# A two-layer hybrid decoder: five reorderings of work around the state-space mixer and the experts

## The chip, the cores and the metric

One Trainium2 chip, one core of it. The metric is the device time of one execution in microseconds. The kernel before takes 1630.93 us, the median of three runs.

## What is computed

A decoder trunk of two layers on 256 tokens of width 1024, in float32. The change touches the second layer, a Mamba-2 mixer and a top-2-of-8 expert layer:

```python
def mamba2_mixer(x, w_in, conv_w, conv_b, dt_bias, a_log, d_skip, norm_w, w_out):
    z, xbc, dt = split_last(x @ w_in, (SSM_D_INNER, SSM_CONV_DIM, SSM_HEADS))
    xbc = jax.nn.silu(causal_depthwise_conv(xbc, conv_w) + conv_b)
    xs, bmat, cmat = split_last(xbc, (SSM_D_INNER, SSM_GROUPS * SSM_STATE, SSM_GROUPS * SSM_STATE))
    ...
    dt = jax.nn.softplus(dt.astype(f32) + dt_bias)
    y = ssd_chunked(xs, dt, -jnp.exp(a_log.astype(f32)), ...)
    y = y + d_skip.astype(f32)[:, None] * xs.astype(f32)
    y = y.reshape(Bsz, T, SSM_D_INNER) * jax.nn.silu(z.astype(f32))
    y = rms_norm(y.reshape(Bsz, T, SSM_GROUPS, -1), norm_w.reshape(SSM_GROUPS, -1)).reshape(Bsz, T, SSM_D_INNER)
    return y.astype(x.dtype) @ w_out
```

The scan runs over two chunks of 128 tokens and four groups of 8 heads. Behind it stand a layer norm, the router, and eight SwiGLU experts of width 3584 whose rows are picked per token.

## The kernel before, in words

Each engine has one instruction stream written out by hand, and the streams wait for one another through semaphores; there is no scheduler. The order in which an engine's work stands in the source is the order in which it runs.

**Weights.** Weights come in pieces of 1 MB (128 x 2048 floats). SP loads a piece into one of six or seven buffers `raw`; ACT casts it to the fp32r type, `w_hi` (`dense_high`, L690); DVE subtracts to make the low half, `w_lo` (`dense_low`, L1112); PE multiplies three times, high by high, high by low, low by high. Three pairs of `w_hi` and `w_lo` exist in the mixers (`CUT`), so ACT may cast piece n once piece n-3 is used (`d_piece_used`), and SP may load piece n once the low half of piece n-6 is made (`d_lo_made`, `RAW_D`). In the experts there are four pairs (the fourth lies in `xT_hi` and `xT_lo`) and seven buffers; there the cast is L936, the low half L1551, the products L2318 to L2320.

**Input projection (`PROJ`, 20 pieces from N1).** Per piece PE runs 48 matmuls of 256 columns (`columns`, L1810 to L1812). Twelve pieces (kind 0) are followed by a depthwise convolution on DVE (L1137, L1141) and a SiLU on ACT (L861), eight (kind 1, the gate) by a SiLU on ACT alone (L864). The order of kinds is 0, 0, 1, 0, 1, four times over. At step 8 (`ACS_AT`) PE sums the decays over the tokens, into bank 7. DVE takes them out of that bank (L1432, L1433, `nacs` and `sdd`), at its own step 8, ahead of that step's low half; PE must not write bank 7 in step 9 before that (`ssm_cols`).

**Scan.** For eight pairs (chunk t, group g) PE makes rows of decay sums (`acs_rows`, L2192 and L2195), ACT their exponentials (`segments`, L881), DVE the product with the chunk's C B matrix (L1477), PE the y of the group (`y_products`, L2207), DVE adds the skip term (L1458) and, in chunk 0, the gate (L1467). ACT copies four states (L892) between the exponentials of groups 0 and 1. Ahead of all that ACT's stream issues two DMAs that fill the slot arrays `x_slots` (4 MB) and `y_slots` (2.5 MB) in DRAM with zeros (L885, L887); only POOL's scatter of tokens, some 130 us later, needs them. DVE makes the low half of the first piece of the output projection, N2, ahead of the product of the third pair.

**Output projection (eight pieces from N2).** For chunk 1 four groups of offsets come from PE (`offset_products`, L2219 and L2221), ACT (`offset_decay`, L902) and DVE (`offset_add`, L1485 to L1490). ACT scales and casts y (`y_high`, L907) and squares it (`y_square`, L914); DVE makes the low part (`y_low`, L1495) and folds the squares (`over_chunks`, L1516, L1517). Two pieces make one group; `y_out(i, t)` is piece i for token tile t, 12 matmuls of 512 columns (L2248 to L2250), and a group's result takes four banks, 4 to 7 for groups 0 and 2, 0 to 3 for groups 1 and 3. The squares are summed by 16 small matmuls (L2260); DVE makes the mean (L1527), POOL its power -1/2 (L649), and DVE adds each group, scaled, to `x_tok` (`group_add`, L1504). In the kernel before PE sums the squares behind group 0 and waits for the mean before group 1, since the sums lie in bank 0. Behind `out_tile` DVE begins the layer norm.

**Experts.** DVE works out each token's slot in the arrays (L1680 to L1692) ahead of the low half of the first expert's fifth piece; POOL scatters the tokens by it (L656, four indirect DMAs), and the other experts read their tokens from `x_slots` (L987). Each expert has seven steps of gate, up and down product; `turn_h` (L2343) transposes h, ACT and DVE copy it as high and low (L969, L1600), `down` multiplies. In the last expert the last `turn_h` stands behind the last but one `down`.

## Time and profile before

| | |
|---|---|
| median of 3 runs | 1630.93 us (1630.56 to 1632.22) |
| profiled execution, its own time | 1623.04 us |
| its span | 1621.2 us |
| PE busy | 1570.1 us, 97% |
| weight loads of PE | 1331.7 us, 82% |
| DVE busy | 1281.6 us, 79% |
| ACT busy | 967.3 us, 60% |
| POOL busy | 54.8 us, 3% |
| moved by DMA | 459.39 MB, 283 GB/s over the span |

Busy time of an engine counts its instructions, not its waits. In the timelines a row is one or several instructions of a line, with start and duration in us; in brackets stand the engine's idle time just before and the instruction that ended it. The granted clock is given as a share of 2.4 GHz; 0.5 is 1.2 GHz. The input projection of the state-space mixer lies at 394 to 522 us, its scan to 570, its output projection to 629, layer norm and router to 650, the experts to 1609.

### The profile page before, as it was taken

What the parts mean: (1) busy time and instruction counts of PE and PEld (TensorE: products, weight loads), DVE (VectorE), ACT (ScalarE), POOL (GpSimd) and SP (SyncE); (2) the same over time, 40 slices, a digit from 0 to 9 for tenths busy, and PEclk for the clock granted to TensorE, in tenths of its full rate; (3) what the DMA queues carried; (4) which work ended last, traced back from release to release, by engine and by line L of the source; (5) the groups of instructions that cost most, each with busy time, mean ns of one, the idle gap of its engine ahead of it and who ended that gap; (6) DMA issues with size and microseconds to landing.
All of it is one profiled execution on the core that took longest, in us unless ns stands there. A gap on an engine that the chain in (4) does not pass through costs nothing.

```text
span 1621.2 us, 22157 instructions
## 1 busy us (share of the span) xinstructions
PE 1570.1 (97%) x8631; PEld 1331.7 (82%) x8631; DVE 1281.6 (79%) x1059; ACT 967.3 (60%) x821; POOL 54.8 (3%) x43
## 2 busy tenths in 40 slices
PE   9989999999989899999999999999999999999996
PEld 7888599998989777788888878888878888888885
DVE  6776545557667587988888888888888889888996
ACT  4414244443434552777777777777767777777773
POOL 3000000002000010100000000000000000000100
PEclk9999999999999999999999999999999999999998
DMA  9150365554543506899999999999999999999991
GB/s 322 61 197 1 128 191 185 194 184 139 173 145 142 196 27 236 308 394 394 395 390 388 381 370 367 384 377 394 376 377 367 386 374 386 387 382 378 393 397 68
DMA packets 221758, 459.39 MB, mean 283 GB/s; under 512 B 7684, under 2 KB 64736, under 8 KB 221664
## 3 DMA queue, kind: packets, MB, share of 16 engines
q1 hardware_dynamic: 208800, 434.95, 73.8%
q10 hardware_dynamic: 11152, 18.42, 3.1%
q0 software_dynamic: 1712, 4.68, 0.8%
q8 instruction: 70, 1.15, 0.3%
q14 instruction: 24, 0.20, 0.0%
HBM read 444.38 MB, written 13.63 MB: 283 GB/s over the span
## 4 chain that ended last, share of the span: by engine, by line
PE 87%; DVE 8%; ACT 2%; issue 1%; ACTq 1%; POOL 0%; DMA 0%; DVEq 0%; SPq 0%
PE ps L2318 19%; PE ps L2320 19%; PE ps L2319 19%; PE ps L1810 5%; PE ps L1811 5%; PE ps L1812 5%; PE ps L1803 2%; PE ps L2343 2%; DVE w_lo L1112 1%; PE ps L2089 1%; PE ps L2090 1%; PE ps L2091 1%; DVE arena L1141 1%; ACT w_hi L690 1%; PE ps L2009 1%
## 5 line engine op out<-in xcount | busy, mean ns | idle before, releaser
L1551 DVE TENSOR_TENSOR w_lo<-raw,w_hi 128x2048 fp32r<-128x2048 f32 x252 | 576.9, 2291 | 71.6 <-ACT w_hi L936 70.7
L936 ACT CAST w_hi<-raw 128x2048 fp32r<-128x2048 f32 x252 | 482.8, 1916 | 132.7 <-PE ps L2320 132.7
L2318 PE MATMUL ps<-w_hi,xg_hi 128*128 128x512 f32 x672 | 267.8, 399 | 6.6 <-DVE w_lo L1551 3.6
L2320 PE MATMUL ps<-w_hi,xg_lo 128*128 128x512 f32 x672 | 262.6, 391 | 0.0
L2319 PE MATMUL ps<-w_lo,xg_hi 128*128 128x512 f32 x672 | 261.8, 390 | 0.0
L1112 DVE TENSOR_TENSOR w_lo<-raw,w_hi 128x2048 fp32r<-128x2048 f32 (+1 forms) x72 | 170.1, 2367 | 112.3 <-ACT w_hi L690 112.3
L1810 PE MATMUL ps<-xT_hi,w_hi 128*128 128x256 f32 x768 | 219.9, 286 | 7.1 <-DVE arena L1433 6.8
L690 ACT CAST w_hi<-raw 128x2048 fp32r<-128x2048 f32 (+1 forms) x72 | 135.3, 1881 | 147.5 <-PE ps L1812 97.1
L1811 PE MATMUL ps<-xT_lo,w_hi 128*128 128x256 f32 x768 | 219.3, 286 | 0.0
L1812 PE MATMUL ps<-xT_hi,w_lo 128*128 128x256 f32 x768 | 219.1, 285 | 0.0
L1551 DVE TENSOR_TENSOR xT_lo<-raw,xT_hi 128x2048 fp32r<-128x2048 f32 x84 | 192.4, 2290 | 30.3 <-ACT xT_hi L936 30.3
L936 ACT CAST xT_hi<-raw 128x2048 fp32r<-128x2048 f32 x84 | 160.8, 1915 | 43.8 <-PE ps L2320 43.8
L1810 PEld LDWEIGHTS ps<-xT_hi,w_hi 128*128 128x128 f32 x768 | 149.2, 194 | 8.6 <-DVE arena L1433 7.0
L2318 PEld LDWEIGHTS ps<-w_hi,xg_hi 128*128 128x128 f32 x672 | 126.3, 188 | 32.4 <-issue 7.5
L1811 PEld LDWEIGHTS ps<-xT_lo,w_hi 128*128 128x128 f32 x768 | 149.2, 194 | 0.4
L1812 PEld LDWEIGHTS ps<-xT_hi,w_lo 128*128 128x128 f32 x768 | 149.3, 194 | 0.0
L2320 PEld LDWEIGHTS ps<-w_hi,xg_lo 128*128 128x128 f32 x672 | 126.2, 188 | 27.3
L2319 PEld LDWEIGHTS ps<-w_lo,xg_hi 128*128 128x128 f32 x672 | 126.6, 188 | 24.4
L2318 PE MATMUL ps<-w_hi,ehT_hi 128*128 128x512 f32 x336 | 131.6, 392 | 1.4 <-DVE ehT_lo L1600 1.4
L2319 PE MATMUL ps<-w_lo,ehT_hi 128*128 128x512 f32 x336 | 130.9, 390 | 0.0
L2320 PE MATMUL ps<-w_hi,ehT_lo 128*128 128x512 f32 x336 | 130.9, 390 | 0.0
L2320 PE MATMUL ps<-xT_hi,xg_lo 128*128 128x512 f32 x224 | 87.3, 390 | 0.0
(396 smaller groups left out, 2165.8 us busy)
## 6 DMA issues: line engine op xcount, KB each, us to landing
raw<-in_moe_w_gate SPq DMA_DIRECT2D x112, 1024.0 KB, 7.6
raw<-in_moe_w_up SPq DMA_DIRECT2D x112, 1024.0 KB, 8.3
raw<-in_moe_w_down SPq DMA_DIRECT2D x112, 1024.0 KB, 8.1
raw<-in_ssm_w_in SPq DMA_DIRECT2D x20, 1024.0 KB, 5.3
raw<-in_ffn_w_gate SPq DMA_DIRECT2D x11, 1024.0 KB, 5.4
raw<-in_ffn_w_up SPq DMA_DIRECT2D x11, 1024.0 KB, 5.4
raw<-in_ffn_w_down SPq DMA_DIRECT2D x11, 1024.0 KB, 4.9
raw<-in_even_w_in SPq DMA_DIRECT2D x10, 1024.0 KB, 13.2
```

The lines of the kernel that those rows point to most:

```text
L690: act.copy(w_hi[:, c, 0:size], raw[:, i, 0:size]).then_inc(sem("dense_hi_made"), 1)
L936: act.copy(e_hi((n + 2 * odd) % CUT_E), raw[:, i, :]).then_inc(sem("hi_made"), 1)
L1112: TTO(w_lo[:, c, 0:size], raw[:, i, 0:size], w_hi[:, c, 0:size].bitcast(F32), ALU.subtract).then_inc(d_lo_made, 1)
L1551: TTO(e_lo(c), raw[:, n % RAW, :], e_hi(c).bitcast(F32), ALU.subtract).then_inc(lo_made, 1)
L1803: last = mm(ps[:, 4 + 2 * t + n, :], mixT[:, k, t * P:(t + 1) * P], w[:, kk, 512 * n:512 * n + 512], start=k == 0, stop=k == KD - 1)
L1810: mm(out_ap, whi, xT_hi[:, k, :], start=first, stop=False)
L1811: mm(out_ap, whi, xT_lo[:, k, :], start=False, stop=False)
L1812: return mm(out_ap, wlo, xT_hi[:, k, :], start=False, stop=last_)
L2318: mm(out_ap, hi, whi, start=start, stop=False)
L2319: mm(out_ap, hi, wlo, start=False, stop=False)
L2320: return mm(out_ap, lo, whi, start=False, stop=stop)
L2343: last = pe.transpose(ps[:, 4, c * P:(c + 1) * P], eh[:, side(j), c * P:(c + 1) * P], ident)
```

## The change

Five things change places; no instruction that computes is added or taken away.

1. DVE takes the column sums out of bank 7 at its step 6 (`COLS_AT`), behind that step's low half.
2. The two clears are issued by SP, behind the sixth load of the output projection, and not by ACT.
3. In the output projection ACT casts pieces N2+1 and N2+2 earlier, the first ahead of all offsets; DVE makes their low halves earlier, folds all squares in one lot, makes the mean, and interleaves the low halves N2+3 and N2+4 with the y low parts of groups 2 and 3. PE runs `y_out(2, 0)` ahead of the sums of squares, which now go to bank 3, and waits for the mean only before the second half of `y_out(2, 1)`.
4. The 15 operations of the slot arithmetic go into the first expert's head in three lots, at its steps 12, 15 and 18 (`slot_rows`, `slot_numbers`, `slot_weights`: the same 15 lines, parted).
5. In the last expert the last `turn_h` stands between the two halves of the last but one `down` (`turn_next`, set for that one alone).

```diff
-DT_AT, SP_AT, DA_AT, ACS_AT = 3, 5, 6, 8
+DT_AT, SP_AT, DA_AT, COLS_AT, ACS_AT = 3, 5, 6, 6, 8
@@ stream of SP @@
             for i in range(N_OUT):
                 n = N2 + i
                 piece(n, n % RAW_D, rows(w_out1, 2 * i, 2))
+                if i == RAW_D - 1:
+                    sp.wait_ge(sem("pool_set"), 2)
+                    sp.dma_start(x_slots[0:E * P, :].rearrange("(p r) (s c) -> p (r s) c", p=P, c=256),
+                                 zerob[:, :].bitcast(F32).unsqueeze(1).to_broadcast([P, 4 * E, 256])).then_inc(sem("slots_cleared"), 16)
+                    sp.dma_start(y_slots[(E - 1) * P:, :].rearrange("(p r) (s c) -> p (r s) c", p=P, c=256),
+                                 zerob[:, :].bitcast(F32).unsqueeze(1).to_broadcast([P, 4 * (1 + 2 * TT), 256])).then_inc(sem("slots_cleared"), 16)
@@ stream of ACT, ahead of the scan @@
-            act.wait_ge(sem("pool_set"), 2)
-            act.dma_start(x_slots[0:E * P, :]
...
-            act.dma_start(y_slots[(E - 1) * P:, :]
@@ stream of ACT, output projection @@
+            act.wait_ge(sem("y_made"), SG)
+            act.wait_ge(sem("xdec_made"), 1)
+            out_high(N2 + 1)
             offset_decay(0)
             offset_decay(1)
             y_high(0)
             y_square(0)
             offset_decay(2)
             y_high(1)
-            out_high(N2 + 1)
             offset_decay(3)
+            act.wait_ge(sem("y_made"), TT * SG)
+            out_high(N2 + 2)
             y_square(1)
             y_high(2)
+            y_square(2)
             y_high(3)
-            y_square(2)
             y_square(3)
-            out_high(N2 + 2)
@@ stream of DVE, input projection @@
-                if m == ACS_AT:
+                n = N1 + m + CUT
+                if n < N2:
+                    dense_low(n, n % RAW_D, n % CUT)
+                if m == COLS_AT:
                     dve.wait_ge(sem("acs_made"), 1)
                     link(TS(nacs[:, :, :], ps[:, 7, 64:64 + TT * SH].rearrange("p (t h) -> p t h", t=TT), -1.0, None, ALU.mult))
                     TTO(sdd[:, :], ps[:, 7, 128:160], nacs[:, 0, :], ALU.add).then_inc(sem("ssm_cols"), 1)
-                n = N1 + m + CUT
-                if n < N2:
-                    dense_low(n, n % RAW_D, n % CUT)
@@ stream of DVE, output projection @@
             offset_add(2)
+            dve.wait_ge(sem("yoff_made"), SG)
+            out_low(N2 + 1)
             offset_add(3)
             y_low(1)
-            out_low(N2 + 1)
...
-            over_chunks(0)
-            over_chunks(1)
+            out_low(N2 + 2)
+            for g in range(SG):
+                over_chunks(g)
+            dve.wait_ge(sem("y_ss"), 1)
+            TS(ymean[:, :], ps[:, 3, 0:TT * SG], 1.0 / (SI // SG), RMS_EPS, ALU.mult, ALU.add).then_inc(sem("y_mean"), 1)
+            out_low(N2 + 3)
             y_low(2)
-            over_chunks(2)
-            over_chunks(3)
+            out_low(N2 + 4)
             y_low(3)
-            out_low(N2 + 2)
-            dve.wait_ge(sem("y_ss"), 1)
-            TS(ymean[:, :], ps[:, 0, 0:TT * SG], 1.0 / (SI // SG), RMS_EPS, ALU.mult, ALU.add).then_inc(sem("y_mean"), 1)
...
+            dve.wait_ge(sem("y_rn"), 1)
+            add_group(0)
+            out_low(N2 + 5)
+            out_low(N2 + 6)
+            dve.wait_ge(sem("y_summed"), 1)
+            add_group(1)
+            out_low(N2 + 7)
@@ stream of DVE, experts @@
-            def expert_head(it, odd, previous, previous_e, back=False):
+            def expert_head(it, odd, previous, previous_e, back=False, first=False):
                 for n in range(START, HEAD_END):
+                    if first and n == START + 8:
+                        slot_rows()
+                    if first and n == START + 11:
+                        slot_numbers()
+                    if first and n == START + 14:
+                        slot_weights()
@@ stream of PE, output projection @@
                 if g == 1:
                     pe.wait_ge(sem("yoff_added"), 4)
+                    y_out(2, 0)
                     pe.wait_ge(sem("ysq_summed"), SG)
                     for t in range(TT):
                         for q in range(SG):
-                            last = mm(ps[:, 0, SG * t + q:SG * t + q + 1], ysq[q][:, t * P:(t + 1) * P], ones[:, 0:1],
+                            last = mm(ps[:, 3, SG * t + q:SG * t + q + 1], ysq[q][:, t * P:(t + 1) * P], ones[:, 0:1],
                                       start=True, stop=True)
                     last.then_inc(sem("y_ss"), 1)
-                    pe.wait_ge(sem("y_mean"), 1)
+                    y_out(2, 1, True).then_inc(d_piece_used, 1)
+                    y_out(3, 0)
+                    y_out(3, 1).then_inc(d_piece_used, 1)
                 if g >= 2:
                     pe.wait_ge(sem("y_summed"), g - 1)
-                if g < SG - 1:
+                if g in (0, 2):
@@ stream of PE, experts @@
                 for half in range(PPU):
+                    if half and turn_next:
+                        turn_h(it, j + 1)
                     pe.wait_ge(lo_made, count(PPE, it, (RAW + n + half + 1)))
...
                 else:
-                    turn_h(it, ESTEPS - 1)
                     down(it, odd, ESTEPS - 1, place(ESTEPS - 1, 2, False), by_half)
```

Three places in the order of the instructions follow, where parts 1 to 3 lie.

DVE in the input projection, before: from the low half of piece N1+9 (step 6) to the convolution of step 8. L1112 is a low half, L1137 and L1141 a convolution, L1432 and L1433 the column sums.

```order
L1112 TENSOR_TENSOR w_lo<-raw,w_hi 128x2048
L1137 TENSOR_SCALAR arena<-ps,pcol 128x256 x2
L1141 SCALAR_TENSOR_TENSOR arena<-ps,pcol,arena 128x255 x2
L1141 SCALAR_TENSOR_TENSOR arena<-ps,pcol,arena 128x254 x2
L1141 SCALAR_TENSOR_TENSOR arena<-ps,pcol,arena 128x253 x2
L1112 TENSOR_TENSOR w_lo<-raw,w_hi 128x2048
L1432 TENSOR_SCALAR arena<-ps 128x64
L1433 TENSOR_TENSOR arena<-ps,arena 128x32
L1112 TENSOR_TENSOR w_lo<-raw,w_hi 128x2048
L1137 TENSOR_SCALAR arena<-ps,pcol 128x256 x2
```

And in the change, where the same lines are L1116, L1141 and L1145, L1439 and L1440:

```order
L1116 TENSOR_TENSOR w_lo<-raw,w_hi 128x2048
L1439 TENSOR_SCALAR arena<-ps 128x64
L1440 TENSOR_TENSOR arena<-ps,arena 128x32
L1141 TENSOR_SCALAR arena<-ps,pcol 128x256 x2
L1145 SCALAR_TENSOR_TENSOR arena<-ps,pcol,arena 128x255 x2
L1145 SCALAR_TENSOR_TENSOR arena<-ps,pcol,arena 128x254 x2
L1145 SCALAR_TENSOR_TENSOR arena<-ps,pcol,arena 128x253 x2
L1116 TENSOR_TENSOR w_lo<-raw,w_hi 128x2048 x2
L1141 TENSOR_SCALAR arena<-ps,pcol 128x256 x2
```

The two rows of the sums moved from behind the second low half to behind the first, ahead of the convolution.

ACT from the copies of the chunk products to the exponentials of the scan, before (L885 and L887 are the clears, L892 the copies of the states):

```order
L872 COPY arena<-ps 128x512 x2
L885 DMA x_slots<-zerob 4096x1x256
L887 DMA y_slots<-zerob 2560x1x256
L881 ACTIVATE arena<-ps,arena 128x128 x8
L892 COPY arena<-ps 128x512 x4
L881 ACTIVATE arena<-ps,arena 128x128 x8
L690 CAST w_hi<-raw 128x2048
L881 ACTIVATE arena<-ps,arena 128x128 x48
```

In the change, and on to the first offsets (L696 is a weight cast, L903 an offset's exponential):

```order
L878 COPY arena<-ps 128x512 x2
L887 ACTIVATE arena<-ps,arena 128x128 x8
L893 COPY arena<-ps 128x512 x4
L887 ACTIVATE arena<-ps,arena 128x128 x8
L696 CAST w_hi<-raw 128x2048
L887 ACTIVATE arena<-ps,arena 128x128 x48
L696 CAST w_hi<-raw 128x2048
L903 ACTIVATE arena<-ps 128x512 x2
L908 ACTIVATE y_hi<-arena,pcol 128x256 x4
```

The clears left ACT's stream, and a weight cast came in between the scan's exponentials and the offsets'.

DVE in the output projection, before, from the fold of the third square to the addition of group 0 (L1495 is y low, L1527 the mean, L1504 the addition):

```order
L1516 TENSOR_TENSOR arena<-arena 128x512
L1517 TENSOR_TENSOR arena<-arena 128x256
L1516 TENSOR_TENSOR arena<-arena 128x512
L1517 TENSOR_TENSOR arena<-arena 128x256
L1495 SCALAR_TENSOR_TENSOR xT_lo<-arena,pcol,y_hi 128x256 x4
L1112 TENSOR_TENSOR w_lo<-raw,w_hi 128x2048
L1527 TENSOR_SCALAR arena<-ps 128x8
L1112 TENSOR_TENSOR w_lo<-raw,w_hi 128x2048 x2
L1504 SCALAR_TENSOR_TENSOR x_tok<-ps,arena,x_tok 128x1024 x2
```

In the change (L1499 is y low, L1527 the mean, L1508 the addition):

```order
L1512 TENSOR_TENSOR arena<-arena 128x512
L1513 TENSOR_TENSOR arena<-arena 128x256
L1512 TENSOR_TENSOR arena<-arena 128x512
L1513 TENSOR_TENSOR arena<-arena 128x256
L1527 TENSOR_SCALAR arena<-ps 128x8
L1116 TENSOR_TENSOR w_lo<-raw,w_hi 128x2048
L1499 SCALAR_TENSOR_TENSOR xT_lo<-arena,pcol,y_hi 128x256 x4
L1116 TENSOR_TENSOR w_lo<-raw,w_hi 128x2048
L1499 SCALAR_TENSOR_TENSOR xT_lo<-arena,pcol,y_hi 128x256 x4
L1508 SCALAR_TENSOR_TENSOR x_tok<-ps,arena,x_tok 128x1024 x2
```

The mean now stands ahead of two low halves and two y low parts that stood in part ahead of it, and the addition of group 0 right behind them.

## Rows read from the trace of the kernel before

**Rows 1.** Busy time by stretch: us, PE, PEld, DVE, ACT, POOL (instructions), PEclk, DMA share, GB/s
```profile
456.00:464.00 8.00, 7.45 (x45) 7.45 (x46) 6.06 (x12) 1.00 (x3) 0.00 (x0) 0.67 0.83 262
...
480.00:522.00 42.00, 42.00 (x352) 42.00 (x352) 30.74 (x46) 15.91 (x19) 0.00 (x0) 1.00 0.43 151
...
586.00:594.00 8.00, 7.46 (x28) 6.06 (x28) 7.86 (x18) 4.12 (x4) 0.00 (x0) 0.79 0.40 131
...
660.00:680.00 20.00, 16.45 (x75) 13.28 (x73) 19.75 (x17) 12.60 (x9) 7.74 (x4) 1.00 0.81 296
...
680.00:700.00 20.00, 20.00 (x92) 16.58 (x91) 18.45 (x10) 14.80 (x10) 0.00 (x0) 1.00 1.03 396
```

**Rows 2.** Timeline of PE at its waits: start us, us, operation [idle before <-releaser]
```profile
456.55 0.58 PE L1810 MATMUL ps<-xT_hi,w_hi 128*128 128x256 f32 x1 [6.76 <-DVE arena L1433]
...
541.05 1.97 PE L2207 MATMUL ps<-arena 128*64 128x128 f32 x16 [5.26 <-ACT arena L892]
...
586.53 0.47 PE L2248 MATMUL ps<-w_hi,y_hi 128*128 128x512 f32 x1 [1.80 <-DVE w_lo L1112]
...
664.42 0.47 PE L2318 MATMUL ps<-w_hi,xg_hi 128*128 128x512 f32 x1 [3.55 <-DVE w_lo L1551]
...
1600.28 0.50 PE L2318 MATMUL ps<-w_hi,ehT_hi 128*128 128x512 f32 x1 [1.40 <-DVE ehT_lo L1600]
```

**Rows 3.** Timeline of DVE in the state-space input projection
```profile
447.50 0.87 DVE L1137 TENSOR_SCALAR arena<-ps,pcol 128x256 f32<-128x256 f32 x2
...
483.17 0.87 DVE L1137 TENSOR_SCALAR arena<-ps,pcol 128x256 f32<-128x256 f32 x2
...
489.53 4.58 DVE L1112 TENSOR_TENSOR w_lo<-raw,w_hi 128x2048 fp32r<-128x2048 f32 x2 [2.77 <-ACT w_hi L690]
```

**Rows 4.** Timeline of ACT behind the copies of the chunk products
```profile
528.65 8.10 ACTq L887 DMA_DIRECT2D y_slots<-zerob  x1
```

**Rows 5.** Timeline of ACT, DVE and PE, second and third scan group
```profile
540.70 2.28 ACT L881 ACTIVATE arena<-ps,arena 128x128 f32<-128x128 f32 x8
...
543.01 1.23 DVE L1477 TENSOR_TENSOR arena<-arena 128x1024 f32<-128x1024 f32 x1 [2.78 <-ACT arena L881]
...
546.03 2.29 DVE L1112 TENSOR_TENSOR w_lo<-raw,w_hi 128x2048 fp32r<-128x2048 f32 x1
...
550.58 1.10 PE L2207 MATMUL ps<-arena 128*64 128x128 f32 x16 [0.18 <-DVE arena L1477]
```

**Rows 6.** Timeline of PE, DVE and POOL in the output projection
```profile
579.00 0.50 PE L2248 MATMUL ps<-w_hi,y_hi 128*128 128x512 f32 x1
...
588.43 1.66 DVE L1495 SCALAR_TENSOR_TENSOR xT_lo<-arena,pcol,y_hi 128x256 fp32r<-128x256 f32 x4
...
593.69 0.50 PE L2260 MATMUL ps<-ones,raw 128*128 128x1 f32 x4
...
596.16 5.84 POOL L649 TENSOR_TENSOR arena<-arena,nhalf 128x8 f32<-128x8 f32 x1 [195.82 <-DVE arena L1527]
...
623.77 1.28 DVE L1504 SCALAR_TENSOR_TENSOR x_tok<-ps,arena,x_tok 128x1024 f32<-128x1024 f32 x1 [3.06 <-PE ps L2250]
```

**Rows 7.** Timeline of DVE ahead of the first expert
```profile
656.80 0.17 DVE L1680 SCALAR_TENSOR_TENSOR rowf<-const,rank 128x16 f32<-128x16 f32 x1
...
659.89 0.17 DVE L1693 TENSOR_SCALAR rank<-rank 128x16 f32<-128x16 f32 x1
```

**Rows 8.** DMA issues, 600 to 720 us: KB each, us to landing; the first token load
```profile
raw<-in_moe_w_gate SPq DMA_DIRECT2D x12, 1024.0 KB, 12.0
...
x_slots<-x_tok,slot_of POOLq DMA_INDIRECT x4, 8.7
...
L987 ACTq DMA_DIRECT2D xg_tok<-x_slots x7: 362/366/367, 732.2 to 1446.2; - x7
```

**Rows 9.** Timeline of DVE and PE at the end of the last expert
```profile
1594.53 0.68 DVE L1596 TENSOR_TENSOR eh<-esg,ps 128x512 f32<-128x512 f32 x1
...
1598.28 0.60 PE L2343 MATMUL ps<-const,eh 128*128 128x128 f32 x4
```

More of the change, by code:

```diff
@@ L2412, in expert_rest @@
                         (turn_tokens if placed else gather)(following)
-                    down(it, odd, j - 1, place(j - 1, 2))
+                    if following is None and j == ESTEPS - 1:
+                        down(it, odd, j - 1, place(j - 1, 2), False, None, True)
+                    else:
+                        down(it, odd, j - 1, place(j - 1, 2))
                     if place(j - 1, 2) + 1 == PLACE_G and not placed:
```

66 lines of the change are left out of this document (30 added, 36 removed).

## Prediction

> **What bounds the kernel now.** I read the busy time by stretch first. Through the projections TensorE is busy for the whole of a stretch [rows 1]: from 480 to 522 us it runs 352 matmuls of 256 columns in 42.00 us, 0.12 us each, so a piece of the projection (48 matmuls) is 5.76 us. So only what holds PE up, or lowers its clock, is worth anything, and I went to its timeline next [rows 2]: five waits of more than a microsecond from 450 us on, each ended by another engine, none by a DMA. Each of the five parts of the change lies at one of them. Then I read what the releasing engine did just before [rows 3 to 9]. The profiled execution took 1623.04 us (span 1621.2); the median of the runs is 1630.93, 7.9 us or 0.5% more, and I subtract the same sum from it. A measurement of this kernel tells 0.2%, 3.3 us, from no change.
>
> **Part 1, the column sums ahead of the convolutions (COLS_AT).** Piece 9 of the projection waits 6.76 us for L1433 [rows 2], since DVE computes it two steps late. In the stretch behind, the granted clock is 0.67 of 2.4 GHz over 8 us [rows 1]: 2.6 us lost, 2.3 of them in matmuls. Loss 9.1 us. In the change DVE does the sums right behind the low half of piece 9, at 447.50 [rows 3], 0.45 us of work for which everything is there, and PE goes on at 449.8. But DVE and ACT hold a loop of their own: convolution, SiLU, cast of the next piece, low half. It takes 6.36 us from the start of a convolution to the next low half (483.17 to 489.53) [rows 3] and 2.2 for that low half (4.58 for two); with a gate piece between, another 2.2 to 2.3. A group of five pieces (three convolutions) so takes the loop 30.3 us and PE 28.8, so the loop decides where PE gains its lead. From 447.95 the low half of piece 10 ends at 447.95+6.36+2.2 = 456.5, PE wants it at 455.5: 1.1 with the signal. The convolutions of pieces 8, 10 and 11 then start at 458.8, 469.65 (10.85 each, with a gate piece between) and 478.2 (8.56), the low half of piece 15 ends at 478.2+8.6 = 486.8, and PE wants it at 456.6 + 5 x 5.76 = 485.4: 1.4. **Part 1 gives 9.1 - 1.1 - 1.4 = 6.6 us.** Bounds: 9.1 if no wait returned, 5 if the loop is 0.5 us slower at each turn.
>
> **Part 2, clearing the slot arrays from SP's queue.** ACT's queue is held for 8.10 us by the issue of the second clear [rows 4]; the exponentials and the state copies stand behind it, and PE waits 5.26 us for the copies [rows 2]. PE had finished the second group's row sums at 535.79. Without the clears ACT's exponentials of group 1 start then, not at 540.70, and take 2.2; DVE's product (543.01 before) starts at 538.15. From that product to PE's third group nothing waits for long: product, additions, gate, the low half of out-piece 0 at 546.03, the next product, 6.5 us in all. So the third group starts at 544.65 and not at 550.58 [rows 5]. **Part 2 gives 5.9 us**, with the half clock there in it. The groups behind keep their spacing, which PE's own work sets. A new PE wait of about 1.9 us stands before the third group: PE has two groups' row sums and two products to do from 535.79, some 6.9 us as I estimate from its work between the waits, and the low half is now late relative to it. On SP the clears go behind the sixth out-piece, issued when the last projection piece's low half is done (some 509 us in the new time). SP is held about 9 us, and its next load needs the low half of out-piece 0, at least 20 us later; the transfers (6.5 MB) lie beside PE work that needs no load. Cost nothing; without that cover, the 9 us.
>
> **Part 3, the output projection.** From 579.00 to the layer norm at 623.77 are 44.8 us [rows 6]. Ten half pieces (12 matmuls) fill 596.2 to 623.6: 2.73 us each. The change casts piece 1 while ACT waited for the offset products, so the wait of 1.80 us for its low half [rows 2] goes, and with it the fall of the clock behind it: 0.79 over 8 us, 3.4 us at 1.2 GHz, 1.7 lost [rows 1]. PE now runs five half pieces (13.65 us) before the sums of squares. From their start, 2.4 us to the mean. DVE then stands before low 3, y low, low 4, y low, addition of group 0: 2.2+1.6+2.2+1.6+2.4 = 10.0 (y low is 1.66, an addition 1.28 a tile) [rows 3, 6], and PE may overwrite group 0's banks 12.5 us after the sums began. It has 1.8 + 3 x 2.73 = 10.0 us of work till then: **a new wait of 2.5 us**. Six half pieces follow, 16.4. Sum 13.65+12.5+16.4+0.2 = 42.8: **part 3 gives 2.0 us**. The mean's power on POOL takes 5.84 us [rows 6]; DVE asks for it 7.6 us after the mean, 1.6 to spare.
>
> **Part 4, the slot arithmetic behind eight pieces of the first expert.** PE waits 3.55 us for the low half of piece 4 [rows 2]. Ahead of it on DVE stand 15 small operations from 656.80 to 659.89 [rows 7]: **3.1 us**, all less than the wait. They come back in three lots, at most 1.5 us, where DVE is idle 1.55 of 20 us [rows 1] and a low half is finished some 4 us before PE takes it. POOL's scatter of the tokens moves from 661 to about 697 us, where the DMA engines are full (share 1.03, 396 GB/s). It writes 2.1 MB, 5.3 us of their time. A load is issued when the low half seven pieces back is done, and its cast starts when the piece four back is used: 7 x 2.8 - 4.2 = 15.4 us, against 12.0 to landing [rows 8]; with the 4 us behind the cast that is 7.4 of slack, so I take nothing. Bounds: 0 and 3.1 lost.
>
> **Part 5, the last transposes between the halves of the last but one product.** After them (1598.28) PE waits 1.40 us for ACT and DVE [rows 2]; now 2.73 us of matmuls lie over that chain. DVE has multiplied the h that they read by 1595.2 [rows 9], and they now come at 1598.28 - 2.73 = 1595.55. **1.4 us**; bounds 1.4 and, if h came later than they do, some tenths less.
>
> **Sum:** 6.6 + 5.9 + 2.0 + 3.1 + 1.4 = 19.0 us. What I take off again is the clock. PE has two new waits, 1.9 and 2.5 us. The old one of 1.80 us was followed by 3.4 us at 1.2 GHz (0.79 in rows 1), the one of 3.55 us was not (1.00 from 660 to 680 us), so either can happen, and I count one of two: 1.7 us. That gives 17.3 us: 1605.7 for a profiled execution, **1613.6 for the median**. [...]
>
> **The rivals.**
> *No fall of the clock behind either new wait*: 19.0 us, 1611.9. For it: the 3.55 us wait. Chance 0.25.
> *Both fall*: 15.6 us, 1615.3. For it: the 1.80 us wait; the first of the new ones lies among short matmuls. 0.15.
> *The gain ahead of the first expert is lost*: scatter and weight loads share full DMA engines and the casts come late, or the lots of small operations delay the low halves. The 5.3 us of the scatter must exceed the slack of 7.4; I may have that slack too large by the few microseconds that loads are late at the start. Time 1613.6 + 3.1 = 1616.7. 0.08. [...]
> *The change moves waits and shortens nothing (1630.9)*: the loop of DVE and ACT would have to take back all of part 1, the third scan group all of part 2. The rows give it 2.5 of 9.1 and 1.9 of 8. 0.03.
> *Slower*: ACT waits at the end of the first expert's first half until all four scatters have landed; the token load behind that wait was issued at 732.2 [rows 8], in the new time near 729 of the old scale. The scatters start near 697, POOL needs 7.7 us for them (rows 1, 660 to 680), and a landing took 8.7: 714, 15 us ahead. Beyond 729 each microsecond stops the casts, and PE with them once its few ready pieces are used. It decides from 15 + 17 = 32 us of added landing time; a landing of 60 us in place of 8.7 would make 1613.6 + 51 - 15 = 1650. No kind of transfer in rows 8 takes more than 12 in the median. 0.02.
>
> **How the numbers follow.** The forecast itself, one of the two falls, has 0.43; 0.04 is left for a gain smaller than all but the last rivals, from a step I mis-sized. The range goes from 1610.6 (no fall, and 1.3 us of rounding in the parts) to 1618.2 (both falls with nearly all of part 4 lost, or part 1 at its lower bound with one fall and part 4 lost). Faster by over 0.2% is the forecast, the first three rivals and the leftover: 0.95. Same 0.03, slower 0.02.
>
> **What would show it.** In the profile after: no PE wait for the column sums, but one near piece 10 and one near piece 15 of the projection, 1.1 and 1.4 us; the projection ends 6 to 7 us earlier; the clear's issue on SP and PE's first scan group behind its row sums without a wait; a wait of about 1.9 us before the third group; in the output projection one wait, 2.5 us, for DVE's L1508 addition, none for the low half of piece 1; at most 0.5 us before piece 4 of the first expert; none behind the last transposes. I am wrong if DVE's loop holds PE at more pieces than two, if the granted clock is below 1 for more than 7 us between 510 and 600 us, if ACT waits for loads in the first expert, or if a scatter lands later than the token load asks for it.

## The result, and the profile after

The changed kernel took **1606.13 us** in the median of four runs (1605.12 to 1610.23), the kernel before, run beside it, 1630.74 (1624.07 to 1632.22). The ratio is 0.9862, with a 95% interval of 0.9829 to 0.9894: faster, as forecast, but by 24.6 us where the forecast had 17.3, and below the low end of the range (1610.6). The profiled execution of the changed kernel took 1607.09 us, that of the kernel before 1623.04: 16.0 less.

| | before | after |
|---|---|---|
| median of the four runs beside each other | 1630.74 | 1606.13 |
| profiled execution, its own time | 1623.04 | 1607.09 |
| its span | 1621.2 | 1605.2 |
| mean granted clock (1 is full speed) | 0.990 | 0.994 |

The longest waits of PE between 440 and 700 us of the changed kernel (engine, line, releaser: us in total, times, longest us):

```profile
PE ps L2228 <- DVE arena L1481: 2.4, 4, 1.8
PE ps L1831 <- DVE w_lo L1116: 2.3, 2, 1.2
PE ps L2271 <- DVE x_tok L1508: 1.9, 1, 1.9
PE ps L1804 <- DVE x_tok L1136: 0.6, 1, 0.6
PE ps L2344 <- DVE w_lo L1557: 0.5, 1, 0.5
```

The waits of 6.76 and 5.26 us and that of 1.80 [rows 2] have no row any more. Where each stands in PE's timeline:

```profile
458.33 0.35 PE L1831 MATMUL ps<-xT_hi,w_hi 128*128 128x256 f32 x1 [1.09 <-DVE w_lo L1116]
...
488.60 0.36 PE L1831 MATMUL ps<-xT_hi,w_hi 128*128 128x256 f32 x1 [1.24 <-DVE w_lo L1116]
...
539.95 1.09 PE L2228 MATMUL ps<-arena 128*64 128x128 f32 x16 [1.81 <-DVE arena L1481]
...
594.16 0.50 PE L2271 MATMUL ps<-w_hi,y_hi 128*128 128x512 f32 x1 [1.87 <-DVE x_tok L1508]
...
648.48 0.47 PE L2344 MATMUL ps<-w_hi,xg_hi 128*128 128x512 f32 x1 [0.48 <-DVE w_lo L1557]
```

They are the two returning waits of part 1 (forecast 1.1 and 1.4), the new one before the third scan group (1.9), the new one before the second half of the output projection (2.5), and what is left of the 3.55 us before piece 4 of the first expert (at most 0.5). Behind the last transposes there is none.

DVE's timeline shows what each new wait waits for. The column sums (L1439, L1440) now stand behind the low half and ahead of the convolution:

```profile
446.98 2.29 DVE L1116 TENSOR_TENSOR w_lo<-raw,w_hi 128x2048 fp32r<-128x2048 f32 x1 [2.38 <-ACT w_hi L696]
449.19 0.22 DVE L1439 TENSOR_SCALAR arena<-ps 128x64 f32<-128x64 f32 x1
449.44 0.19 DVE L1440 TENSOR_TENSOR arena<-ps,arena 128x32 f32<-128x32 f32 x1
...
533.46 1.22 DVE L1481 TENSOR_TENSOR arena<-arena 128x1024 f32<-128x1024 f32 x1 [4.43 <-ACT arena L887]
...
536.47 2.29 DVE L1116 TENSOR_TENSOR w_lo<-raw,w_hi 128x2048 fp32r<-128x2048 f32 x1
538.68 1.22 DVE L1481 TENSOR_TENSOR arena<-arena 128x1024 f32<-128x1024 f32 x1
```

The clear now stands in SP's queue, and the next load comes long after it:

```profile
511.32 11.02 SPq L539 DMA_DIRECT2D y_slots<-zerob  x1
538.79 0.37 SPq L493 DMA_DIRECT2D raw<-in_ssm_w_out  x1
```

The clear holds SP for 11.0 us (8.10 on ACT before [rows 4]), free of cost, since 16 us lie between its end and the next load. The granted clock by stretch (us, PE, PEld, DVE, ACT, POOL with instructions, PEclk, DMA share, GB/s), first before the third scan group, then at the output projection's new wait, then where part 4 lies:

```profile
534.00:542.00 8.00, 6.01 (x64) 5.20 (x64) 7.86 (x14) 5.47 (x17) 0.00 (x0) 1.00 0.24 79
...
594.00:602.00 8.00, 7.84 (x34) 6.49 (x35) 6.96 (x6) 2.19 (x2) 0.00 (x0) 1.00 0.01 2
...
644.00:664.00 20.00, 19.52 (x88) 15.88 (x87) 19.75 (x17) 15.69 (x12) 0.00 (x0) 1.00 0.90 327
```

The clock fell behind neither new wait in this execution, nor anywhere else from 400 us to the last 10 us. PE is busy 19.52 of 20 us ahead of and in the first expert, where it was 16.45 [rows 1].

**Where the 16 us came from.** I took the start of the same matmul in both timelines, counted from the first matmul of the input projection (393.72 before, 395.41 after), so that what happens ahead of it is left out:

| to the start of | before | after | saved in this stage | forecast |
|---|---|---|---|---|
| last matmul of the projection | 127.97 | 121.69 | 6.3 (part 1) | 6.6 |
| third scan group | 156.86 | 144.54 | 6.0 (part 2) | 5.9 |
| first expert | 255.97 | 241.41 | 2.2 (part 3) | 2.0 |
| piece 4 of the first expert | 270.70 | 253.07 | 3.1 (part 4) | 3.1 |
| last expert matmul | 1211.46 | 1193.75 | 0.1 | 1.4 (part 5) |

The first four parts gave 17.6 us, which is their forecast to the tenth. The wait of part 5 is gone (1.40 us), yet its stage gained 0.1: the expert loop took 1.3 us more in this execution. And the projection itself began 1.7 us later. Neither lies at an edit. The loop is where the prediction's list of waits is short by two: the trace of the kernel before has, besides its five, idle times of 1.52 and 1.16 us at the two returns of the expert loop, which no engine ends; the changed kernel has 2.29 and 2.03 us there. So the mechanisms stood, and three questions were left: how large the change is if not 24.6 or 16.0, what moves a run by several microseconds, and whether the two new waits are worth removing.

### The profile page after: what moved, and what is told of

The parts are those of the page before. It is cut to its first block, busy times and chain, and to the rows that moved or that the text cites. A ratio compares the mean times of both kernels' runs of the same rounds, so it can differ in the third digit from the quotient of the medians.

```text
span 1605.2 us, 22159 instructions
## 1 busy us (share of the span) xinstructions
PE 1564.3 (97%) x8630; PEld 1325.9 (83%) x8631; DVE 1278.9 (80%) x1059; ACT 967.2 (60%) x821; POOL 55.1 (3%) x43
## 4 chain that ended last, share of the span: by engine, by line
PE 86%; DVE 9%; ACT 2%; issue 1%; POOL 0%; DMA 0%; DVEq 0%; SPq 0%; ACTq 0%
PE ps L2344 19%; PE ps L2346 19%; PE ps L2345 19%; PE ps L1831 4%; PE ps L1833 4%; PE ps L1832 4%; DVE w_lo L1116 2%; PE ps L1824 2%; PE ps L2369 2%; DVE arena L1145 1%; PE ps L2111 1%; PE ps L2110 1%; PE ps L2112 1%; ACT w_hi L696 1%; DVE w_lo L1557 1%
## 5 line engine op out<-in xcount | busy, mean ns | idle before, releaser
L1116 DVE TENSOR_TENSOR w_lo<-raw,w_hi 128x2048 fp32r<-128x2048 f32 (+1 forms) x72 | 168.4, 2344 | 107.1 <-ACT w_hi L696 107.0
L696 ACT CAST w_hi<-raw 128x2048 fp32r<-128x2048 f32 (+1 forms) x72 | 135.3, 1879 | 142.7 <-PE ps L1833 93.3
L2345 PEld LDWEIGHTS ps<-w_lo,xg_hi 128*128 128x128 f32 x672 | 126.4, 188 | 24.6
```

Of the source, the lines that this page charges most:

```text
L696: act.copy(w_hi[:, c, 0:size], raw[:, i, 0:size]).then_inc(sem("dense_hi_made"), 1)
L1116: TTO(w_lo[:, c, 0:size], raw[:, i, 0:size], w_hi[:, c, 0:size].bitcast(F32), ALU.subtract).then_inc(d_lo_made, 1)
L2345: mm(out_ap, hi, wlo, start=False, stop=False)
```

## The experiments

Each kernel was run beside the kernel before on the same chip. The parts are numbered as in the prediction.

| run | what | median | before, median | ratio, 95% interval | gain |
|---|---|---|---|---|---|
| a_same | the kernel before itself | 1628.73 | 1628.31 | 1.0004 (0.9982 to 1.0026) | -0.4 |
| a_all | whole change | 1610.43 | 1628.31 | 0.9891 (0.9865 to 0.9918) | 17.9 |
| a_p12 | parts 1 and 2 | 1618.55 | 1628.31 | 0.9937 (0.9918 to 0.9956) | 9.8 |
| a_p3 | part 3 | 1627.49 | 1628.31 | 0.9990 (0.9971 to 1.0008) | 0.8 |
| b_all | whole change again | 1608.48 | 1628.99 | 0.9863 (0.9836 to 0.9890) | 20.5 |
| b_p45 | parts 4 and 5 | 1623.53 | 1628.99 | 0.9961 (0.9943 to 0.9978) | 5.5 |
| b_fill | before, 27 fillers | 1628.66 | 1628.99 | 0.9996 (0.9980 to 1.0013) | 0.3 |
| b_both | change, two waits removed | 1604.26 | 1628.99 | 0.9845 (0.9818 to 0.9872) | 24.7 |
| c_p1245 | all but part 3 | 1611.76 | 1627.48 | 0.9895 (0.9877 to 0.9912) | 15.7 |
| c_both | as b_both | 1606.17 | 1627.48 | 0.9861 (0.9839 to 0.9883) | 21.3 |
| c_fill3 | before, fillers in three waits | 1639.39 | 1627.48 | 1.0060 (1.0040 to 1.0079) | -11.9 |
| d_pad | before, 54 short fillers | 1640.21 | 1629.27 | 1.0061 (1.0040 to 1.0082) | -10.9 |

### The kernel before, and the whole change, twice

No edit in the first; the whole diff in the other two.

> The kernel before, unchanged, once more. The medians lie 24.6 us apart (1630.74 and 1606.13), the two profiled executions 16.0 (spans 1621.2 and 1605.2), and my parts sum to 19.0. Theory C (the clock's falls are a lottery that the kernel before draws more often, since it has more and longer waits of TensorE): its executions spread over some 8 us, and the span falls with the mean granted clock: 1 us of span for each 0.0006 of clock (1.2 us at half clock cost 0.6). At 1631 us the clock must then be near 0.985, at 1623 near 0.990. Rival S (something else in the timed executions, such as slower DMA in the experts): the clock is the same, 0.990, at 1631 as at 1623.

> The whole change once more. Theory C: times between 1603 and 1610, the clock 0.992 to 0.995, the fastest those with no fall of the clock in the second layer; the profile again has two waits in the input projection (1.1 and 1.2 us), one of 1.8 before the third scan group and one of 1.9 before group 2 of the output projection. Rival S: times vary with an unchanged clock.

> The whole change again, for its distance from the kernel before in another draw. Theory C (every execution draws its own falls of TensorE's clock; the parts of the change shorten 19 us of work and waits in all of them): the median lies 16 to 20 us below that of the kernel before, ratio 0.988 to 0.990, as in the first batch (17.9). Theory T (the parts save more than the profiles show, and the 24.6 us between the first two medians are their true size): 23 to 26 us, ratio 0.984 to 0.986. In the profile the five waits of the kernel before are gone under both, and the stretch from the first projection matmul of layer 2 to the last expert matmul is 17 to 20 us shorter.

The same program spread over 15 us: 72 runs of the kernel before in the four batches went from 1622.88 to 1637.79, median 1628.5, mean 1629.0, standard deviation 3.3. (The twelve runs of a_same, not among them, went from 1623.84 to 1640.99; that last one has a granted clock of 0.932, which fits neither its time nor any other run, and stays unexplained.) The twelve of the changed kernel went from 1603.71 to 1616.61, median 1609.9, mean 1609.7, deviation 3.1. The means are 19.3 us apart (95% interval 17.4 to 21.2), near the sum of the parts' terms in the prediction (19.0) and neither 24.6 (theory T) nor 16.0. The medians, 17.9 and 20.5 us apart, lie about it; the second is half a microsecond beyond theory C's range and far from T's. Theory C had 1603 to 1610 us for a_all; four of its six runs lie above, up to 1611.54. A run's time goes with its clock, as theory C has it and rival S has not: of the kernel before 0.990 at 1622.88 us, 0.987 at 1628.31, 0.983 at 1637.79, and over the 72 runs 1.6 us for each 0.001 of clock. But the clock isn't all: runs at one clock, 0.985, lie between 1627.83 and 1636.40.

One program's executions differ in where the clock falls. The whole change with its new waits as in the first execution, but now with some 3.4 us at half clock behind each of them (0.79 over 8 us; same columns as above):

```profile
536.00:544.00 8.00, 6.20 (x53) 5.44 (x51) 6.70 (x13) 3.01 (x12) 0.00 (x0) 0.79 0.41 133
592.00:600.00 8.00, 6.14 (x21) 4.88 (x21) 8.00 (x6) 1.90 (x1) 0.00 (x0) 0.79 0.01 2
```

The waits ahead of them were 1.80 and 1.86 us, against 1.81 and 1.87 in the profile without a fall. From the first projection matmul to piece 4 of the first expert that execution took 256.3 us and not 253.1. The kernel before shows the same: 0.57 behind the 6.76 us wait and 0.79 behind the one of 3.55 us in its second profile, where the first had 0.67 and 1.00 [rows 1]:

```profile
456.00:464.00 8.00, 4.51 (x23) 4.51 (x24) 7.12 (x10) 3.03 (x3) 0.00 (x0) 0.57 0.46 146
666.00:674.00 8.00, 5.57 (x18) 4.53 (x19) 8.00 (x5) 1.99 (x2) 6.60 (x4) 0.79 0.70 216
```

So whether half clock follows a wait of 1.8 to 3.6 us changes from execution to execution. The same reading for the fourteen traces of this study, from the clock that each of them records (one trace per kernel, so these are counts and no rates):

| idle time of PE | traces in which it stands | of these with half clock at its end (begun up to 3 us before or 1.5 us after) |
|---|---|---|
| 6.76 us, column sums | 4 | 4, 6.8 us each |
| 3.55 us, piece 4 of the first expert | 7 | 6, four times 6.8 us and twice 3.4 |
| 1.80 us, out-piece 1 | 7 | 3, 3.4 us each |
| 1.8 us, third scan group (new) | 5 | 2, 3.4 us each |
| 1.87 us, before the addition's banks (new) | 4 | 2, 3.4 us each |

The 3.55 us wait is the one that matters. The first profile of the kernel before is the only one of the seven in which nothing follows it. From piece 4 to the first idle time of the expert loop PE takes 304.4 us in all eight traces without that fall, 305.8 and 305.9 with 3.4 us of it, 307.0 to 307.2 with 6.8: the fall costs 1.4 or 2.6 to 2.8 us.

At out-piece 1 it costs nothing. From there to the first matmul of group 1 PE takes 9.61 or 9.62 us in all eight traces with the old order, with the fall or without it, since that matmul waits for DVE's mean either way. With the fall (the first trace, the kernel before) this second wait is 0.62 us, without it (the second, b_p45) 1.87:

```profile
596.15 0.48 PE L2248 MATMUL ps<-w_hi,y_hi 128*128 128x512 f32 x1 [0.62 <-DVE arena L1527]
```

```profile
598.19 0.48 PE L2263 MATMUL ps<-w_hi,y_hi 128*128 128x512 f32 x1 [1.87 <-DVE arena L1527]
```

Not every fall stands behind a wait. In seven of the fourteen traces the clock falls between 415.6 and 417.9 us, where PE's last idle time, 0.68 us, lies over 20 us back; in c_both for 6.8 us, with PE busy throughout:

```profile
416.00:424.00 8.00, 8.00 (x45) 8.00 (x45) 5.13 (x10) 3.19 (x4) 0.00 (x0) 0.58 0.42 131
```

That lies in the input projection, ahead of all edits. A projection with 3.4 us of it ends 1.2 to 1.6 us later behind its start, the one of c_both 3.1 us; neither profile of the first comparison had it.

### The parts

The edit of each is its hunks of the diff: the COLS_AT ones and the clears (a_p12), the output projection's (a_p3), the slot arithmetic's and the last transposes' (b_p45), and all but the output projection's (c_p1245).

> Parts 1 and 2 alone (column sums at step 6, clears from SP). By the rows 6.6 + 5.9 = 12.5 us less than before in a profiled execution with the same falls elsewhere. Theory C: about 4 to 8 us more than that in the medians, since the two longest waits (6.76 and 5.26) go; some 16 to 20 in all. Rival S: 12.5 in the medians too.

> Part 3 alone (the order in the output projection). By the rows 2.0 us less, 1.7 of it a fall of the clock that goes: the new wait before group 2 is 1.9 to 2.5 us. Theory C: 0 to 3.7 us less, by whether the clock falls behind the new wait. Rival: part 3 gains nothing alone, since the new wait takes the place of the two old ones.

> Parts 4 and 5 alone (slot arithmetic behind eight pieces of the first expert, the last transposes between the halves). By the steps of the prediction 3.1 + 1.4 = 4.5 us, ratio 0.9972. Theory C: 4 to 6 us, since a fall can follow the 3.55 us wait too (it did in one profile of the kernel before). Rival G (the scatter of the tokens beside the weight loads takes part of it back in the expert loop, as the two longer gaps at 952 and 1192 us of the changed kernel's profile could be read): 1.5 to 3 us, with those gaps longer than in the kernel before of the same batch.

> All parts but the output projection's. By the steps of the prediction 6.6 + 5.9 + 3.1 + 1.4 = 17.0 us. Measured singly so far: parts 1 and 2 9.8 us, parts 4 and 5 5.5 us, part 3 0.8 us, which add to 16.1 where the whole change gave 17.9 and 20.5. If the parts simply add: 15.3 us, ratio 0.9906, and the medians so far are scattered about one size. If a fall saved at one wait comes back at the next wait that is left (theory R), taking parts together gives more than their sum: 17 to 19 us, ratio 0.9884 to 0.9896.

By medians, parts 1 and 2 gave 9.8 where the sum has 12.5 and where I had expected 16 to 20: a miss. Parts 3 to 5 came within 1.2 us of their terms, but part 3 alone isn't told from nothing (0.8 us, interval of the ratio 0.9971 to 1.0008). Rival G falls: the interval of parts 4 and 5 is 3.6 to 9.3 us, its forecast was 1.5 to 3. Medians of some ten runs that spread like these carry about a microsecond each, so I also took means, each against the mean of the kernel before in its batch: 10.4, 2.2 and 5.8, together 18.4 beside 19.3 for the whole; without part 3 it is 17.1 (1611.9 in the mean of five runs), with 17.0 forecast. Within this scatter the parts add; the idea that a fall saved at one wait returns at the next, and that only the whole gains, isn't needed, but it isn't excluded: for c_p1245 it had 17 to 19 us, where the median has 15.7 and the mean 17.1. In a_p12's profile the stages hold what they do in the whole change (121.7 us to the last projection matmul), and what is missing lies behind: half clock from 539.7, 577.3, 652.4, 963.0 and 1205.3 us.

### Filling the waits

The first edit, in the kernel before; the second adds the two other places:

```diff
                 if kind == 1 and q == 3:
+                    pe.wait_ge(sem("ssm_conv"), 3)
+                    keep_running(2, 27)
                     pe.wait_ge(sem("ssm_cols"), 1)
```

```diff
+            pe.wait_ge(sem("cb_copied"), TT)
+            keep_running(2, 21)
             for i in range(TT * SG):
...
+                        if i == 1:
+                            pe.wait_ge(sem("er_made"), 4)
+                            keep_running(3, 6)
                         y_out(i, 0)
```

> The kernel before with 27 matmuls of 512 columns (into a bank that nothing reads again) in the 6.76 us that piece 9 waits for the column sums, so that the wait stays and PE is busy in it. It prices the fall of the clock apart from the wait. Theory C: the fall follows the idle time, so the granted clock in the 8 us behind piece 9's start is 1 and not 0.67, and the median falls by 2.3 to 3.4 us (ratio 0.998 to 0.9985) with the wait itself unchanged. Rival R (falls come at their own times, or one saved here only turns up at the next wait): clock below 1 in the 8 us behind or one more fall soon after, median within 1 us of the kernel before.

> The kernel before with PE kept busy in three of its waits: 27 filler matmuls in the 6.76 us before piece 9, 21 in the 5.26 us before the first scan product, 6 in the 1.80 us before out-piece 1. The waits and everything that is computed stay. Theory C (falls of the clock are worth what the rows say, 2.0 to 2.6, 1.0 to 1.6 and 1.7 us): no fall from 450 to 600 us, median 4.7 to 5.9 us below the kernel before, ratio 0.9964 to 0.9971; the missing clock (1 - granted clock, times the span) falls by 5 us or more. Theory R (the falls move to the next wait, here the 3.55 us one of the first expert): median within 1.5 us of the kernel before, with a fall of 6.8 us behind the 3.55 us wait in the profile.

The fillers do what they should to the clock. In the four traces in which the 6.76 us wait is idle 6.8 us at half clock follow it; in the three in which it is filled (b_fill, c_fill3 and d_pad, below) none do, so this fall follows the idle time. With 27 the stretch behind the wait stands at 1.00, and the projection ends 125.9 us behind its start and not 128.0: 2.0 us is what the fall costs there. But behind the 3.55 us wait, untouched, that execution fell to 0.59 where the first had 1.00:

```profile
456.00:464.00 8.00, 7.07 (x54) 6.01 (x52) 7.86 (x12) 2.02 (x2) 0.00 (x0) 1.00 0.61 193
664.00:672.00 8.00, 7.21 (x20) 5.71 (x21) 7.85 (x5) 1.66 (x1) 5.26 (x3) 0.59 0.80 254
```

From the projection on that execution has 17.1 us at half clock before its last 10 us, as the first profile of the kernel before has. The median gained 0.3 us, which is rival R's forecast (within 1 us) and misses theory C's 2.3 to 3.4; but its interval (-2.1 to 3.3) holds most of that range too, and in the mean of twelve runs the missing clock (1 less the granted clock, times the run's time) is 17.8 us and not 21.5, so part of the saved fall does stay away. It isn't settled. With three waits filled the kernel was 11.9 us **slower**, which no theory had. The first 700 us were no slower, but no faster either: 255.95 us to the first expert, 255.97 before, where theory C wanted 4.7 to 5.9 less. The clock is at 1.00 behind the first two filled waits; this execution falls instead at 417 us (3.4 us, no wait near) and at 598 us, behind the wait for the mean. The loss lies in the expert loop, which nothing had touched. At its first return PE shows, in that kernel:

```profile
976.58 0.49 PE L2325 MATMUL ps<-w_hi,xg_hi 128*128 128x512 f32 x1 [1.86 <-DVE w_lo L1551]
...
982.66 0.59 PE L2326 MATMUL ps<-w_lo,xg_hi 128*128 128x512 f32 x1 [3.22 <-issue]
```

and in the kernel before only:

```profile
970.39 0.49 PE L2318 MATMUL ps<-w_hi,xg_hi 128*128 128x512 f32 x1 [1.52 <-issue]
```

A second gap, in which PE waits for no engine, a few matmuls into the loop. Over 18 us about the return the kernel before has 16.48 us of PE and a clock of 1.00, this one 12.92 and 0.72:

```profile
966.00:984.00 18.00, 16.48 (x75) 13.33 (x74) 14.26 (x8) 12.34 (x8) 0.00 (x0) 1.00 1.01 370
```

```profile
972.00:990.00 18.00, 12.92 (x44) 9.86 (x44) 8.54 (x5) 6.34 (x5) 0.00 (x0) 0.72 0.81 303
```

That PE waits there for its own instructions was a guess of mine, which no row shows; it pointed at the fillers' number and not at what they do.

### The same number of instructions, no more time

```diff
+                    pe.wait_ge(sem("ssm_conv"), 3)
+                    for _ in range(54):
+                        mm(ps[:, 2, 0:256], identb[:, :], over_heads(identb[:, :], 2), start=True, stop=True)
                     pe.wait_ge(sem("ssm_cols"), 1)
```

(and the two waits of the former kernel, without their fillers)

> The filling of three waits made the kernel 11.9 us slower, nearly all of it in the two returns of the expert loop (two gaps of PE at each, the second 4.7 and 4.9 us with no releaser, and 10.2 and 6.8 us at half clock), though nothing in that loop was edited. This kernel has the same 54 extra matmuls and the same extra waits ahead of the loop, but all 54 (at 256 columns, half as long) in the 6.76 us before piece 9 alone, as long in all as the 27 that cost nothing. Theory L (the place of the loop in PE's instruction stream sets how long PE stands at each return while its instructions are fetched behind full weight loads): the loop loses the same, median 1636 to 1641 us, ratio 1.005 to 1.008, two gaps at each return. Theory F (what the fillers do to the clock or to the order of the engines, not their number, cost it): as with 27 fillers, 1626 to 1630 us, ratio 0.998 to 1.001, one gap at each return.

1640.21 us, 10.9 above the kernel before: where theory L had it, and not theory F. Its fillers last as long as the 27 did that cost nothing. The same two gaps stand at the return:

```profile
977.21 0.79 PE L2324 MATMUL ps<-w_hi,xg_hi 128*128 128x512 f32 x1 [2.57 <-DVE w_lo L1551]
...
983.56 0.54 PE L2325 MATMUL ps<-w_lo,xg_hi 128*128 128x512 f32 x1 [3.01 <-issue]
```

The second gaps are 3.22 and 3.66 us in c_fill3 (the expectation's 4.7 and 4.9 are more than the idle time of these rows) and 3.01 and 3.93 here. With the first gaps PE stands for 5.1 to 5.6 us at each return of these two kernels, and for 1.1 to 3.8 us in the twelve other traces, b_fill's among them. So it is the 54 extra matmuls with the added waits ahead of the loop that cost 11 us, most of it at the two returns, and not what they do to the clock at the three waits. What isn't separated is their number from the three added semaphore waits, which both kernels have and b_fill has only one of, or from where exactly the loop comes to lie. That PE stands there because its instructions are being fetched, as theory L has it, is not shown: the rows name no releaser, and the DMA view lists an "instruction" packet of 0.02 MB in each 6 us there, in the kernel before as in these two, so it doesn't tell them apart. Measured are the second gaps, 3.0 to 3.9 us, and about the first return a DMA share of 0.81 over 18 us in both kernels, where the kernel before has 1.01 and no second gap.

### The two new waits removed

```diff
+            dense_high(N2, N2 % RAW_D, out_c(N2), N2 // RAW_D + 1)
             segments(0)
...
             segments(1)
-            dense_high(N2, N2 % RAW_D, out_c(N2), N2 // RAW_D + 1)
...
-                if i == 2:
+                if i == 1:
                     dve.wait_ge(sem("state_made"), SG)
                     dense_low(N2, N2 % RAW_D, out_c(N2))
...
             out_low(N2 + 4)
-            y_low(3)
...
             add_group(0)
+            y_low(3)
             out_low(N2 + 5)
```

> The whole change with its two new waits taken away: the cast and the low half of the first out-piece stand ahead of the first scan group (ACT is idle 1.6 us there and DVE 4.4) and not ahead of the third, and the addition of group 0 goes ahead of the last y low. If the two waits are true losses (1.81 and 1.87 us), the third scan group starts 1.8 us earlier behind the first and the addition ends 1.6 us earlier: 3.4 us below the whole change. Theory C adds that a fall of the clock behind either wait can no longer happen: another 0 to 3.4 in the median, so 3.4 to 6.8 below, ratio to the kernel before 0.985 to 0.987. Rival D (DVE is the bound of both stretches, and the moved low half and y low come back as waits before a later group or piece): within 1 us of the whole change.

> The version with the two new waits taken away, again, in another draw. In the last batch 24.7 us below the kernel before (0.9845) and 4.2 below the whole change. If that is its size: 23 to 26 us, ratio 0.984 to 0.986. If it was the draw and only the 3.4 us of the two waits are its own, over the whole change's 19 us: 21.5 to 23 us, ratio 0.986 to 0.987.

The low half lies in DVE's idle time now, and the addition ahead of the last y low:

```profile
530.16 1.23 DVE L1481 TENSOR_TENSOR arena<-arena 128x1024 f32<-128x1024 f32 x1 [2.70 <-ACT arena L887]
531.32 2.29 DVE L1116 TENSOR_TENSOR w_lo<-raw,w_hi 128x2048 fp32r<-128x2048 f32 x1
535.74 1.23 DVE L1481 TENSOR_TENSOR arena<-arena 128x1024 f32<-128x1024 f32 x1 [2.12 <-ACT arena L887]
...
590.87 2.47 DVE L1508 SCALAR_TENSOR_TENSOR x_tok<-ps,arena,x_tok 128x1024 f32<-128x1024 f32 x2
593.26 1.66 DVE L1499 SCALAR_TENSOR_TENSOR xT_lo<-arena,pcol,y_hi 128x256 fp32r<-128x256 f32 x4
```

PE's third scan group starts without a wait (at 540.42 us), and of the wait for the addition 0.28 us is left:

```profile
593.39 0.50 PE L2271 MATMUL ps<-w_hi,y_hi 128*128 128x512 f32 x1 [0.28 <-DVE x_tok L1508]
```

Rival D falls: 4.2 us below the whole change in the first batch. The two batches (11 runs) have a mean of 1605.9 us, 3.9 below the whole change's 1609.7 (95% interval 1.3 to 6.4), with 3.4 from the waits themselves. The traces agree: b_both reaches its first expert 239.8 us behind the start of the projection, the changed kernel 241.4, although b_both had the fall at 417 us and the other hadn't. The 24.7 of the first batch was in part the draw, as the second with 21.3 says. This is the fastest of the kernels run.

## Why the prediction was right or wrong

- **Part 1 (6.6)**: right, 6.3 between the two profiles. The loop of DVE and ACT brings back two waits and no more, 1.09 and 1.24 us. By the timed runs of parts 1 and 2 alone (forecast 12.5) the gain is 9.8 in the median and 10.4 in the mean.
- **Part 2 (5.9)**: right, 6.0, with the 1.81 us wait before the third group. The clear holds SP for 11.0 us, not 9, under the same cover.
- **Part 3 (2.0)**: right in size, 2.2, but two steps of it missed. The new wait is 1.87 us and not 2.5: DVE needs the 10.0 us for its chain, but the mean comes 1.9 us behind the start of the sums (582.11 to 583.99) and not 2.4. And the fall behind the 1.80 us wait, priced at 1.7 us, costs nothing: where it is absent, PE waits 1.87 and not 0.62 us for the mean (9.61 us from out-piece 1 to group 1 either way). The sum of this part is not hurt, since it was made from whole stages.
- **Part 4 (3.1)**: right, 3.1; 0.48 us of wait is left. The scatters started at 686.31 and landed in 9.2 us in the median, and the token load behind them was issued at 716.28, so neither the third rival nor the slower one came near.
- **Part 5 (1.4)**: the wait is gone. That it shortens the kernel by 1.4 us wasn't measured by itself; its stage gained 0.1 in the profile, with 1.6 us more of idle time at the loop's returns. Parts 4 and 5 together gave 5.5 us with 4.5 forecast.
- **The step that failed is the term of the clock: "What I take off again is the clock", 1.7 us, with the falls of the kernel before read from one execution.** The falls behind the new waits were counted right: 0, 2 and 1 in the three traces of the whole change, one of two on average, some 1.6 us each. What was mis-sized is what the change takes away. The prediction has the 3.55 us wait followed by no fall ("the one of 3.55 us was not"), and counts its 3.1 us of wait alone. Half clock follows that wait in six of the seven traces in which it stands, for 1.4 us or 2.6 to 2.8 of lost time, 1.9 us in the mean of the seven. The execution that the prediction was read from is the one without; it has five stretches at half clock before its end, the second trace of the same kernel seven. In the means over the runs the missing clock is 21.5 us before and 12.5 after, 9.0 less; in that first execution the falls from the projection on, all of which the change removes, are 8.5 by the same measure, and the deduction leaves 6.8. So the falls that go outweigh those that come by more than was allowed, and the forecast gain of 17.3 stands against 19.3 measured (17.4 to 21.2): 2.0 too small, just outside the interval. That the 1.9 us make up this difference (17.3 + 1.9 = 19.2) is an estimate from one trace per kernel.
- **The starting point** was the median of three runs, 1630.93, where 72 runs have 1628.5: 2.4 us too high. And the four runs of the result, at 1606.13, are 3 us below the 1609.2 that all sixteen runs of the changed kernel have. The 7.5 us between forecast and result are 2.0 for the gain, 2.4 for the start and 3.1 for the draw. More than half of the miss so is chance on both sides of the comparison; the four runs have 10.0 us of missing clock, the other twelve 12.5.
- **The range** held the parts' bounds and nothing for the draw. Medians of four, drawn from the 84 runs of the kernel before, lie between 1626.7 and 1631.1 in 8 of 10 draws; those of the changed kernel spread about as much. The rival "no fall behind either new wait" was the nearest with 19.0, by luck: its reason, no falls, held in one trace of three.

What stays open: how much of the 19.3 us is time at half clock. The list of PE's idle times is 12.9 us shorter in the changed kernel's first profile (19.4 us before: the five waits and 0.62 for the mean; 6.5 after), which leaves some 6 us for the clock, as an estimate; the experiment that should price it moved the expert loop in PE's instruction stream. Open too is whether the change itself moved the loop (PE stands at its returns for 1.2 to 1.5 us in the first trace of the kernel before, for 1.5 to 3.8 us in the three of the changed one), and why the clock falls at 417 us.

## What to carry to other kernels

Follow each removed wait to the next one on the same engine before you count it: here that was right to 0.6 us at five places. Read more than one execution before you count the falls of the clock, and look whether the next wait swallows a fall before you price it. Then look at how far the runs of the kernel spread before giving a range: with a deviation of 3.3 us, a median of three or four runs is uncertain by 2, on both sides of the comparison, and parts of a few microseconds need ten runs or more, or the distance between the same two instructions in two traces. An engine that is about to idle is a place to put another engine's late work (the low half into DVE's 4.43 us), and a filler that keeps the clock up need not be free: 27 matmuls in one wait changed the median by 0.3 us, 54 in three waits made it 11.9 us longer, by the loop behind them in the stream.

## What the runs showed of the hardware that was not expected

- The same wait is followed by half clock in one execution and not in the next: 1.81 and 1.80 us before the third scan group, 1.00 and 0.79 over 8 us; 3.55 us, 1.00, 0.59 over 8 us (b_fill) and, with 3.54 us in a_same, 0.79. Half clock also came at 415.6 to 417.9 us in seven of fourteen traces, over 20 us behind PE's last idle time. The 6.76 us wait was followed by 6.8 us at half clock in four traces of four, and by none in three of three once matmuls filled it.
- The same 3.4 us at half clock cost 1.4 us behind the 3.55 us wait and nothing behind the 1.80 us one, where the next wait, for DVE, shrank from 1.87 to 0.62 us.
- 54 more matmuls (and three semaphore waits) in PE's stream ahead of a loop made the kernel 11 us slower in the median, through a second gap of 3.0 to 3.9 us at each of its two returns that waits for no engine, and the half clock about it, in two kernels whose fillers differ in size and in part in place.
